# Final norm of a one-core kernel: the addition of the loaded rows moved from VectorE to TensorE, with unread products ahead of it

## The chip, the cores and the metric

The kernel runs on one core of one Trainium2 chip. The metric is the device time of one execution in microseconds (us). The median of three runs before the change is 2208.36 us.

## What is computed

The kernel computes one layer (an mLSTM and a differential attention side by side, then a mixture of 32 experts) over 1024 rows of 1024 numbers, and a final norm. Only the end matters here:

```python
h = h + moe(u2, ...)              # sum over four experts a row of gate * (act @ w_down[e] + b_down[e])
return rms_norm(h, final_g)

def rms_norm(x, g):
    xf = x.astype(jnp.float32)
    y = xf * lax.rsqrt(jnp.mean(xf * xf, axis=-1, keepdims=True) + EPS)
    return (y * g.astype(jnp.float32)).astype(x.dtype)
```

All inputs and the output are float32.

## The kernel before

The 1024 rows are cut into eight tiles (t = 0 to 7) of 128 rows. The products of the experts, without the bias of the second matrix, are added by indirect DMAs from GpSimd into the buffer `h_dram` in memory. That bias is left to the very end: for a row it is the sum over the experts of gate times `b_down[e]`, which is a product with the gates of the row.

The end of the program has two blocks. In the last lines of TensorE's part of `experts` eight transposes (L2278) bring the gates into PSUM, ScalarE copies them to SBUF (L2417), and TensorE makes the bias sums of tiles 0 and 1 (`last_biases`, L2667). A bias sum has only 32 rows of the array in use, one for each expert; it is two float32 products of 512 columns, one for each half of the 1024 columns of a tile, and each shows as two records in the trace. Then comes a barrier of all engines (L1978), which also waits for GpSimd to see its last addition into `h_dram` landed.

In `final_norm`, behind the barrier, SyncE issues the loads of all eight tiles of `h_dram` into `h_all` (L2583). The bias sums of up to four tiles stand in PSUM (`sums`, the four pairs of banks, which are all of PSUM); TensorE makes those of tiles 2 to 7, and from tile 4 on each waits until VectorE has read the sums four tiles earlier. For each tile VectorE adds the bias sums to the loaded rows (L2612, `add`), ScalarE squares and sums the rows (L2594) and takes the root (L2596), VectorE takes the reciprocal (L2619) and multiplies the rows by it and by `final_g` (L2621), and SyncE stores the tile (L2586). VectorE's order is add(0), add(1), scale(0), add(2), scale(1), and so on.

Of the kernel before, what the change touches and what calls it, by code (L numbers as in the profile page):

```python
# [11 lines left out]
ACT = mybir.ActivationFunctionType  # L12
ALU = mybir.AluOpType
X = mybir.AxisListType.X

P = 128
SEQ = 1024
D_MODEL = 1024
NT = SEQ // P
# [1230 lines left out]
class Kit:  # L1250
# [6 lines left out]
    def sb(self, name, shape, dt=F32):  # L1257
        return self.ctx.enter_context(self.nc.sbuf_tensor(name, shape, dt))
# [689 lines left out]
def experts(nc, k):  # L1948
# [29 lines left out]
    with ExitStack() as c:  # L1978
        sb = lambda n, s, d=F32: c.enter_context(nc.sbuf_tensor(n, s, d))
        ps = lambda n, s: c.enter_context(nc.psum_tensor(n, s, F32))  # L1980
        bias, raw = k.bias, k.raw
# [17 lines left out]
        ah, al = sb("ah", [P, KT, P], F32R), sb("al", [P, KT, P], F32R)  # L1999
# [13 lines left out]
        a_ps = ps("a_ps", [P, 2, 512])  # L2013
# [116 lines left out]
        def _(pe):  # L2130
            pe.sem_inc(parts_used.sem, parts_used.credit)
            def turn(b):
                for n in range(KT):
                    last = pe.transpose(x_ps[:, n, :], xg[b][:, n * P:(n + 1) * P], k.c["ident"])
                last.then_inc(x_turned.sem, 1)
# [5 lines left out]
            def turn_act(i, g, blocks):  # L2141
                pe.wait_ge(act_ready.sem, act_ready.at(i, g + 1))
                pe.wait_ge(a_low.sem, a_low.at(i, g))
                to = turned if blocks == 1 else x_ps
                for n in range(2 * blocks):
                    last = pe.transpose(to[:, n, :], av[g % 2][:, n * P:(n + 1) * P], k.c["ident"])
                last.then_inc(act_turned.sem, 1)

            def biases(i, g, blocks):
                if g < 2:  # L2150
                    pe.wait_ge(y_read.sem, y_read.at(i, g - 1))
                elif blocks == 2:
                    pe.wait_ge(gate_ready.sem, gate_ready.at(i, g - 1))
                else:
                    pe.wait_ge(gu_read.sem, gu_read.at(i, g - 1))

                for b in range(blocks if g < 4 else 0):
                    pe.matmul(acc[g % 2][b][:, :], sel[:, b, :], bias[:, g * 512:(g + 1) * 512], start=True, stop=False)
# [63 lines left out]
            def products(i, ch, blocks):  # L2222
                if HALF_OF[ch] == 0:
                    biases(i, GROUP_OF[ch], blocks)
                last = first_block(i, ch)
                if blocks == 2:
                    last = second_block(ch)
                last.then_inc(parts_used.sem, 1)

            def item(i, blocks):  # L2230
                pe.wait_ge(x_low.sem, x_low.at(i, 0))
                if blocks == 2:
                    pe.wait_ge(xg_loaded[1].sem, xg_loaded[1].at(i, 16))
                    turn(1)
                else:
                    pe.sem_inc(x_turned.sem, 1)
                pe.wait_ge(sel_ready.sem, sel_ready.at(i, 1))
                if blocks == 2:

                    biases(i, 0, blocks)  # L2240
                    for ch in range(2):
                        first_block(i, ch)
                    pe.wait_ge(x_low.sem, x_low.at(i, 1))
                    for ch in range(2):
                        second_block(ch).then_inc(parts_used.sem, 1)
                    by_weights(i, 2)
                    turn_act(i, 0, blocks)
                    for ch in range(3, 8):
                        by_weights(i, ch)
                else:  # L2250
                    pe.sem_inc(tiles_made.sem, tiles_made.per)
                    for ch in range(8):
                        products(i, ch, blocks)
                        if ch >= 3 and ch % 2 == 1:
                            turn_act(i, (ch - 3) // 2, blocks)
                pe.wait_ge(a_low.sem, a_low.at(i, 2))
                products(i, 8, blocks)
                if blocks == 2:
                    pe.wait_ge(gu_read.sem, gu_read.at(i, 3))
                turn_next(i)  # L2260
                products(i, 9, blocks)
                if blocks == 1:
                    turn_act(i, 3, blocks)
                products(i, 10, blocks)
                products(i, 11, blocks)
                if blocks == 2:
                    pe.sem_inc(act_turned.sem, 3)
# [9 lines left out]
            for t in range(NT):  # L2277
                last = pe.transpose(x_ps[0:N_EXPERTS, t, :], k.gates[:, t * N_EXPERTS:(t + 1) * N_EXPERTS], k.c["ident"])  # L2278
            last.then_inc(k.half_pe, 1)
            pe.wait_ge(k.half_act, 4)  # L2280
            pe.wait_ge(k.fg_loaded.sem, k.fg_loaded.at(0, 32))
            pe.wait_ge(y_read.sem, y_read.at(items, 0))
            for t in range(2):
                last_biases(pe, k, k.sums[:, 2 * t:2 * t + 2, :], t)

        @block.scalar
        def _(act):
# [273 lines left out]
def final_norm(nc, k, out):  # L2561

    S = k.steps
    h_loaded, squares, root, rstd_ready, normed = k.norm_steps
    stored = S("out_stored", 16)
    g_loaded, fg = k.fg_loaded, k.final_g
    with ExitStack() as c:
        sb = lambda n, s, d=F32: c.enter_context(nc.sbuf_tensor(n, s, d))
        ht = sb("h_all", [P, NT, D_MODEL])
        ot = sb("out_all", [P, NT, D_MODEL])  # L2570
        ssq = sb("f_ssq", [P, NT])
        rms = sb("f_rms", [P, NT])
        rstd = sb("f_rstd_col", [P, NT])
        more = c.enter_context(nc.psum_tensor("more_sums", [P, 4, 512], F32))
        sums = [k.sums[:, 0:2, :], k.sums[:, 2:4, :], more[:, 0:2, :], more[:, 2:4, :]]

        made, added = (lambda t: 4 + t), (lambda t: 4 + t)
        block = c.enter_context(nc.Block(no_gpsimd_drain=True))

        @block.sync  # L2580
        def _(sp):
            for t in range(NT):
                sp.dma_start(ht[:, t, :], k.h_dram[t * P:(t + 1) * P, :]).then_inc(h_loaded[t].sem, 16)  # L2583
            for t in range(NT):
                sp.wait_ge(normed.sem, normed.at(1, t + 1))
                sp.dma_start(out[t * P:(t + 1) * P, :], ot[:, t, :]).then_inc(stored.sem, 16)  # L2586
            sp.wait_ge(stored.sem, stored.at(0, 16 * NT))

        @block.scalar
        def _(act):  # L2590
            nc.scalar.preload_act_table(ACT.Sqrt)
            for t in range(NT):
                act.wait_ge(k.half_dve, added(t))
                nc.scalar.activation(ot[:, t, :], ht[:, t, :], ACT.Square, accum_out=ssq[:, t:t + 1]).then_inc(squares.sem, 1)  # L2594
                act.wait_ge(squares.sem, squares.at(1, t + 1))
                nc.scalar.activation(rms[:, t:t + 1], ssq[:, t:t + 1], ACT.Sqrt, scale=1.0 / D_MODEL,  # L2596
                                     bias=k.eps[:, 0:1]).then_inc(root.sem, 1)

        @block.tensor
        def _(pe):  # L2600
            for t in range(2, NT):
                if t >= len(sums):
                    pe.wait_ge(k.half_dve, added(t - len(sums)))
                last_biases(pe, k, sums[t % len(sums)], t)

        @block.vector
        def _(dve):
            def add(t):
                dve.wait_ge(h_loaded[t].sem, h_loaded[t].at(1, 16))
                dve.wait_ge(k.half_pe, made(t))  # L2610
                rows = ht[:, t, :].rearrange("p (a b) -> p a b", b=512)
                dve.tensor_tensor(rows, sums[t % len(sums)], rows, ALU.add).then_inc(k.half_dve, 1)  # L2612

            dve.wait_ge(g_loaded.sem, g_loaded.at(0, 32))
            add(0)
            add(1)
            for t in range(NT):
                dve.wait_ge(root.sem, root.at(1, t + 1))
                dve.reciprocal(rstd[:, t:t + 1], rms[:, t:t + 1]).then_inc(rstd_ready.sem, 1)  # L2619
                dve.wait_ge(rstd_ready.sem, rstd_ready.at(1, t + 1))  # L2620
                dve.scalar_tensor_tensor(out=ot[:, t, :], in0=ht[:, t, :], scalar=rstd[:, t:t + 1], in1=fg[:, :],  # L2621
                                         op0=ALU.mult, op1=ALU.mult).then_inc(normed.sem, 1)
                if t + 2 < NT:
                    add(t + 2)


def back(nc, k, out):
# [34 lines left out]
def last_biases(pe, k, out, t):  # L2662


    for half in range(2):
        at = slice(half * 512, half * 512 + 512)
        last = pe.matmul(out[:, half, :], k.gates_turned[:, t * P:(t + 1) * P], k.b_down[:, at], start=True, stop=True)  # L2667
    last.then_inc(k.half_pe, 1)


def lay_out(inputs):
# [72 lines left out]
```

## Time and profile before

| what | value |
|---|---|
| median of three runs | 2208.36 us |
| the three runs | 2207.04, 2212.03, 2208.36 us |
| the profiled execution, its own time | 2210.34 us |
| span of the profiled execution, first to last instruction | 2208.3 us |
| mean granted TensorE clock over the span | 0.978 |
| TensorE busy over the span | 97% |
| final block, from the barrier's end to the end of the span | 2179.99 to 2208.3 us |

The span is 2.0 us shorter than the own time of the same execution. A granted clock of 1.00 is 2.4 GHz, one of 0.50 is 1.2 GHz; these are the two levels that the trace shows. An x behind a group is the number of its records.

### The profile page before, as it was taken

What the parts mean: (1) busy time and instruction counts of PE and PEld (TensorE: products, weight loads), DVE (VectorE), ACT (ScalarE), POOL (GpSimd) and SP (SyncE); (2) the same over time, 40 slices, a digit from 0 to 9 for tenths busy, and PEclk for the clock granted to TensorE, in tenths of its full rate; (3) what the DMA queues carried; (4) which work ended last, traced back from release to release, by engine and by line L of the source; (5) the groups of instructions that cost most, each with busy time, mean ns of one, the idle gap of its engine ahead of it and who ended that gap; (6) DMA issues with size and microseconds to landing.
All of it is one profiled execution on the core that took longest, in us unless ns stands there. A gap on an engine that the chain in (4) does not pass through costs nothing. (4 is left out here: it accounts for less than half of the span.)

```text
span 2208.3 us, 35903 instructions
## 1 busy us (share of the span) xinstructions
PE 2133.2 (97%) x11230; PEld 1811.5 (82%) x11231; DVE 1706.5 (77%) x2127; ACT 1373.6 (62%) x1752; POOL 408.2 (18%) x436
## 2 busy tenths in 40 slices
PE   7999999988959999999999999999999999999998
PEld 7987777767848998898898898988889998889884
DVE  5426667776658777979979978779997778998897
ACT  4324655544447566757857757567775667776675
POOL 0000000002342121213213213212321222221120
PEclk9999999999969999999999999999999999999996
DMA  4111101207859776979979979669997769998897
GB/s 162 44 48 34 58 34 44 101 31 229 181 185 343 248 241 248 377 265 349 382 263 353 377 259 352 236 243 380 373 382 267 252 229 332 388 364 336 290 370 283
DMA packets 106797, 548.41 MB, mean 248 GB/s; under 512 B 18071, under 2 KB 28824, under 8 KB 51834
## 3 DMA queue, kind: packets, MB, share of 16 engines
q1 hardware_dynamic: 88138, 504.89, 61.2%
q0 software_dynamic: 18608, 42.85, 8.1%
q8 instruction: 31, 0.51, 0.1%
q14 instruction: 20, 0.16, 0.0%
HBM read 516.45 MB, written 41.47 MB: 253 GB/s over the span
## 5 line engine op out<-in xcount | busy, mean ns | idle before, releaser
L2431 DVE TENSOR_TENSOR wl<-raw,wh 128x2048 fp32r<-128x2048 f32 x423 | 959.1, 2287 | 44.0 <-PE sums L2188 26.8
L2292 ACT ACTIVATE wh<-raw 128x2048 fp32r<-128x2048 f32 x425 | 804.7, 1912 | 113.2 <-PE sums L2188 39.4
L2172 PE MATMUL sums<-wh,xx 128*128 128x512 f32 x832 | 325.8, 392 | 0.9 <-issue 0.9
L2171 PE MATMUL sums<-wl,xx 128*128 128x512 f32 x832 | 325.6, 391 | 0.0
L2170 PE MATMUL sums<-wh,xx 128*128 128x512 f32 x832 | 325.3, 391 | 0.0
L2103 POOL DMA_INDIRECT h_dram<-y,pairs_mine x47 | 120.8, 2570 | 769.1 <-DVE y L2525 449.2
L2170 PE MATMUL sums<-wh,al 128*128 128x512 f32 x560 | 226.7, 405 | 0.6 <-DVE al L2516 0.3
L2172 PE MATMUL sums<-wh,ah 128*128 128x512 f32 x560 | 219.1, 391 | 0.0
L2171 PE MATMUL sums<-wl,ah 128*128 128x512 f32 x560 | 218.5, 390 | 0.0
L2171 PEld LDWEIGHTS sums<-wl,xx 128*128 128x128 f32 x832 | 156.9, 189 | 34.0
L2172 PEld LDWEIGHTS sums<-wh,xx 128*128 128x128 f32 x832 | 156.7, 188 | 33.4
L2170 PEld LDWEIGHTS sums<-wh,xx 128*128 128x128 f32 x832 | 157.1, 189 | 32.4 <-issue 1.2
L2216 PE MATMUL sums<-xx,wh 128*128 128x384 f32 x576 | 172.2, 364 | 0.0
L2217 PE MATMUL sums<-xx,wl 128*128 128x192 f32 x576 | 144.8, 251 | 0.0
L2172 PEld LDWEIGHTS sums<-wh,ah 128*128 128x128 f32 x560 | 105.1, 188 | 23.1
L2170 PEld LDWEIGHTS sums<-wh,al 128*128 128x128 f32 x560 | 105.2, 188 | 21.4 <-DVE al L2516 2.5
L2171 PEld LDWEIGHTS sums<-wl,ah 128*128 128x128 f32 x560 | 105.5, 188 | 19.0
L131 PE MATMUL unit_ps<-u_high,wc_l 128*128 128x512 f32 x288 | 118.5, 411 | 0.9 <-PEq L215 0.9
L2339 ACT ACTIVATE tg<-tg 128x256 f32<-128x256 f32 (+2 forms) x140 | 64.6, 461 | 88.0 <-DVE tg L2450 71.4
L2216 PE MATMUL a_ps<-xx,wh 128*128 128x384 f32 x384 | 114.4, 363 | 0.0
L133 PE MATMUL unit_ps<-u_high,wc_h 128*128 128x512 f32 x288 | 112.9, 392 | 0.0
L132 PE MATMUL unit_ps<-u_low,wc_h 128*128 128x512 f32 x288 | 112.4, 390 | 0.0
(402 smaller groups left out, 4174.6 us busy)
## 6 DMA issues: line engine op xcount, KB each, us to landing
raw<-in_w_experts SPq DMA_DIRECT2D x426, 1024.0 KB, 6.5
raw<-in_w_chan SPq DMA_DIRECT2D x20, 512.0 KB, 3.3
o_gate<-in_x SPq DMA_DIRECT2D x8, 512.0 KB, 5.9
raw<-in_w_out SPq DMA_DIRECT2D x8, 512.0 KB, 5.5
ht<-in_x SPq DMA_DIRECT2D x8, 512.0 KB, 5.9
h_dram<-ht SPq DMA_DIRECT2D x8, 512.0 KB, 9.0
u_dram<-ut SPq DMA_DIRECT2D x8, 512.0 KB, 10.1
h_all<-h_dram SPq DMA_DIRECT2D x8, 512.0 KB, 6.8
```

Source lines behind the costliest of these rows:

```text
L131: pe.matmul(out, ll, rh, start=start, stop=False)
L132: pe.matmul(out, lh, rl, start=False, stop=False)
L133: return pe.matmul(out, lh, rh, start=False, stop=stop)
L2103: pool.indirect_dma_start(out=k.h_dram, out_offset=bass.IndirectOffsetOnAxis(ap=mine[rows, b, 0:1].bitcast(U32), axis=0), in_=y[rows, b, : ...
L2170: pe.matmul(out, lo[:, n, :], w_hi[:, kk, :], start=g >= 4 and n == 0, stop=False)
L2171: pe.matmul(out, hi[:, n, :], w_lo[:, kk, :], start=False, stop=False)
L2172: last = pe.matmul(out, hi[:, n, :], w_hi[:, kk, :], start=False, stop=half == 1 and kk == 3)
L2216: pe.matmul(out[:, 0:2 * ROWS], w_hi[:, kk, own], xx[:, n, :], start=n == 0, stop=False)
L2217: last = pe.matmul(out[:, 0:ROWS], w_lo[:, kk, own], xx[:, n, 0:ROWS], start=False, stop=n == KT - 1)
L2292: nc.scalar.activation(wh[ch % HIGHS][:, :, :], raw[ch % RAW][:, :, :], ACT.Copy).then_inc(h_split.sem, 1)
L2339: nc.scalar.activation(t, t, ACT.Silu, scale=ALPHA).then_inc(sig_ready.sem, 1)
L2431: dve.tensor_tensor(wl[ch % LOWS][:, :, :], raw[ch % RAW][:, :, :], wh[ch % HIGHS][:, :, :], ALU.subtract).then_inc(l_split.sem, 1)
```

## The change

TensorE, not VectorE, adds the loaded rows to the bias sums: the sums are left open (`stop=False`), and for each half of a tile a product of the identity matrix with 512 columns of the loaded rows is added into the same PSUM bank (`add_rows`). ScalarE and VectorE then read the finished rows out of PSUM. The addition on VectorE is gone, and `h_all` is only loaded, no longer written back. A pair of PSUM banks is free for the bias sums of a later tile only when VectorE has scaled the tile (`normed`), not when it has been added. In front of the barrier TensorE gets 10 products behind the gates' transposes and 16 behind the bias sums of tiles 0 and 1, whose result nobody reads (`keep_busy`).

```diff
+            def keep_busy(n):
+
+                for _ in range(n):
+                    pe.matmul(a_ps[:, 1, :], ah[:, 0, :], bias[:, 0:512], start=True, stop=True)
...
             last.then_inc(k.half_pe, 1)
+            keep_busy(10)
             pe.wait_ge(k.half_act, 4)
...
             for t in range(2):
                 last_biases(pe, k, k.sums[:, 2 * t:2 * t + 2, :], t)
+            keep_busy(16)
...
             for t in range(NT):
-                act.wait_ge(k.half_dve, added(t))
-                nc.scalar.activation(ot[:, t, :], ht[:, t, :], ACT.Square, accum_out=ssq[:, t:t + 1]).then_inc(squares.sem, 1)
+                act.wait_ge(k.half_pe, made(t))
+                nc.scalar.activation(ot[:, t, :], rows(t), ACT.Square, accum_out=ssq[:, t:t + 1]).then_inc(squares.sem, 1)
...
-            for t in range(2, NT):
-                if t >= len(sums):
-                    pe.wait_ge(k.half_dve, added(t - len(sums)))
-                last_biases(pe, k, sums[t % len(sums)], t)
+            def add_rows(t):
+
+                pe.wait_ge(h_loaded[t].sem, h_loaded[t].at(1, 16))
+                for half in range(2):
+                    last = pe.matmul(sums[t % len(sums)][:, half, :], k.c["ident"], ht[:, t, half * 512:half * 512 + 512],
+                                     start=False, stop=True)
+                last.then_inc(k.half_pe, 1)
+
+            for t in range(2, len(sums)):
+                last_biases(pe, k, sums[t], t)
+            for t in range(NT):
+                add_rows(t)
+                if 1 <= t <= NT - len(sums):
+                    pe.wait_ge(normed.sem, normed.at(1, t))
+                    last_biases(pe, k, sums[t - 1], t - 1 + len(sums))
...
-            add(0)
-            add(1)
             for t in range(NT):
                 dve.wait_ge(root.sem, root.at(1, t + 1))
                 dve.reciprocal(rstd[:, t:t + 1], rms[:, t:t + 1]).then_inc(rstd_ready.sem, 1)
                 dve.wait_ge(rstd_ready.sem, rstd_ready.at(1, t + 1))
-                dve.scalar_tensor_tensor(out=ot[:, t, :], in0=ht[:, t, :], scalar=rstd[:, t:t + 1], in1=fg[:, :],
+                dve.scalar_tensor_tensor(out=ot[:, t, :], in0=rows(t), scalar=rstd[:, t:t + 1], in1=fg[:, :],
                                          op0=ALU.mult, op1=ALU.mult).then_inc(normed.sem, 1)
-                if t + 2 < NT:
-                    add(t + 2)
...
     for half in range(2):
         at = slice(half * 512, half * 512 + 512)
-        last = pe.matmul(out[:, half, :], k.gates_turned[:, t * P:(t + 1) * P], k.b_down[:, at], start=True, stop=True)
-    last.then_inc(k.half_pe, 1)
+        pe.matmul(out[:, half, :], k.gates_turned[:, t * P:(t + 1) * P], k.b_down[:, at], start=True, stop=False)
```

How the instructions of TensorE stand at the end of `experts`, between the gates' transposes (`x_ps`) and the barrier's branch, before (-) and after (+); `b_down` and `raw` (the turned gates) are the operands of the bias sums, and L2667 has become L2676:

```order
-L2276 ISA
-L2278 MATMUL x_ps<-cons,gates 32x128 x8
-L2282 REGISTER_ALU
-L2667 MATMUL sums<-b_down,raw 128x512 x4
+L2281 ISA
+L2283 MATMUL x_ps<-cons,gates 32x128 x8
+L2233 MATMUL a_ps<-bias,ah 128x512 x10
+L2288 REGISTER_ALU
+L2676 MATMUL sums<-b_down,raw 128x512 x4
+L2233 MATMUL a_ps<-bias,ah 128x512 x16
```

The unread products (`a_ps`) stand on both sides of the four bias products. Next, TensorE in `final_norm`, from the barrier's branch on, the first rows of the new order (`cons` holds the identity, `h_all` the loaded rows):

```order
 L1978 UNCONDITIONAL_BRANCH
-L2599 UNCONDITIONAL_BRANCH
-L2667 MATMUL more_sums<-b_down,raw 128x512 x4
-L2667 MATMUL sums<-b_down,raw 128x512 x4
-L2667 MATMUL more_sums<-b_down,raw 128x512 x4
-L2567 UNCONDITIONAL_BRANCH
+L2607 UNCONDITIONAL_BRANCH
+L2676 MATMUL more_sums<-b_down,raw 128x512 x4
+L2613 MATMUL sums<-h_all,cons 128x512 x4
+L2676 MATMUL sums<-b_down,raw 128x512 x2
+L2613 MATMUL more_sums<-h_all,cons 128x512 x2
+L2676 MATMUL sums<-b_down,raw 128x512 x2
```

Twelve products have become 28: the same twelve bias products, and sixteen identity products (L2613) between and behind them; the bias sums of tile 4 stand behind the rows of tile 1 and ahead of the rows of tile 2. Last, VectorE at the end of `final_norm` before, and at its start after:

```order
-L2612 TENSOR_TENSOR h_all<-more_sums,h_all 128x1024
-L2619 RECIPROCAL f_rstd_col<-f_rms 128x1
-L2621 SCALAR_TENSOR_TENSOR out_all<-h_all,f_rstd_col,final_g 128x1024
-L2619 RECIPROCAL f_rstd_col<-f_rms 128x1
-L2621 SCALAR_TENSOR_TENSOR out_all<-h_all,f_rstd_col,final_g 128x1024
-L2567 UNCONDITIONAL_BRANCH
+L2625 UNCONDITIONAL_BRANCH
+L2630 RECIPROCAL f_rstd_col<-f_rms 128x1
+L2632 SCALAR_TENSOR_TENSOR out_all<-sums,f_rstd_col,final_g 128x1024
+L2630 RECIPROCAL f_rstd_col<-f_rms 128x1
+L2632 SCALAR_TENSOR_TENSOR out_all<-sums,f_rstd_col,final_g 128x1024
```

VectorE has lost the eight additions and reads PSUM in the scaling.

## Rows read from the trace of the kernel before

**Rows 1.** The chain that ended last, in order of time: start us, us, what.

```profile
2180.03 7.16 PE more_sums L2667 x8
2187.19 6.83 PE sums L2667 x8
2194.02 6.84 PE more_sums L2667 x8
...
2200.95 1.24 DVE h_all L2612
...
2202.21 1.16 ACT out_all L2594 x2
...
2203.92 1.28 DVE out_all L2621
```

**Rows 2.** Stretches: us, PE, PEld, DVE, ACT, POOL busy; granted clock, DMA share, GB/s.

```profile
2169.20:2173.40 4.20, 1.52 (x10) 0.97 (x9) 3.29 (x2) 3.43 (x4) 2.43 (x1) 1.00 0.04 18
2173.50:2179.60 6.10, 6.10 (x8) 1.89 (x6) 0.00 (x0) 0.00 (x0) 0.56 (x1) 0.50 0.55 86
2179.00:2180.00 1.00, 0.60 (x1) 0.00 (x0) 0.00 (x0) 0.01 (x1) 0.00 (x0) 0.50 0.00 0
2180.00:2200.90 20.90, 20.81 (x24) 7.80 (x24) 16.33 (x19) 11.27 (x22) 0.00 (x0) 0.50 0.87 326
```

**Rows 3.** Timeline from the gates' transposes on: start us, us, engine, group [idle before].

```profile
2169.21 1.03 PE L2278 MATMUL x_ps<-cons,gates 128*32 128x128 f32 x8
2170.97 3.09 POOL L2103 DMA_INDIRECT h_dram<-y,pairs_mine  x1 [13.56 <-ACT y L2360]
2172.92 6.67 PE L2667 MATMUL sums<-b_down,raw 32*128 32x512 f32 x8 [2.68 <-ACT raw L2417]
2175.13 0.33 PEld L2667 LDWEIGHTS sums<-b_down,raw 32*128 32x128 f32 x1 [0.53 <-issue]
2175.99 0.33 PEld L2667 LDWEIGHTS sums<-b_down,raw 32*128 32x128 f32 x1 [0.53 <-issue]
2180.00 3.80 SPq L2583 DMA_DIRECT2D h_all<-h_dram  x8
2183.78 2.44 DVE L2612 TENSOR_TENSOR h_all<-sums,h_all 128x1024 f32<-128x1024 f32 x2 [11.29 <-PE more_sums L2667]
```

**Rows 4.** Last indirect addition (L2103) of the end: time to landing.

```profile
DMA to landing us min/median/max: 7.6/7.6/7.6
```

**Rows 5.** Timeline of two earlier stretches, TensorE alone.

```profile
502.34 0.63 PE L133 MATMUL o_ps<-wo_h,mh 128*128 128x512 f32 x1
502.77 0.63 PE L131 MATMUL o_ps<-wo_h,ml 128*128 128x512 f32 x1
...
504.66 0.40 PE L133 MATMUL o_ps<-wo_h,mh 128*128 128x512 f32 x1
504.89 0.39 PE L131 MATMUL o_ps<-wo_h,ml 128*128 128x512 f32 x1
```

**Rows 6.** Float32 products on 128 rows, at the two levels of the clock.

```profile
478.77 1.72 PE L848 MATMUL sk_ps<-tok,pdT 128*128 128x128 f32 x14
484.65 3.78 PE L848 MATMUL sk_ps<-tok,pdT 128*128 128x128 f32 x16 [0.69 <-ACT pdT L950]
```

**Rows 7.** Stretches between earlier changes of the clock, columns as in rows 2.

```profile
494.20:500.90 6.70, 0.00 (x0) 0.00 (x0) 2.57 (x4) 2.52 (x3) 0.00 (x0) 0.50 0.62 168
501.00:504.30 3.30, 2.95 (x7) 2.40 (x8) 3.30 (x5) 2.46 (x4) 0.00 (x0) 0.50 0.93 324
504.40:507.70 3.30, 3.30 (x16) 2.71 (x15) 3.30 (x4) 3.30 (x4) 0.00 (x0) 1.00 1.08 398
511.20:514.60 3.40, 2.70 (x12) 1.89 (x11) 1.29 (x2) 0.85 (x1) 1.23 (x1) 1.00 0.82 157
514.60:517.90 3.30, 1.45 (x6) 1.21 (x7) 1.23 (x1) 0.16 (x1) 3.10 (x4) 1.00 0.28 103
518.10:521.40 3.30, 3.30 (x10) 2.53 (x9) 1.60 (x2) 1.09 (x3) 3.23 (x2) 0.50 0.99 399
```

**Rows 8.** Groups by line and form that read PSUM: busy us, mean ns.

```profile
L2306 ACT ACTIVATE xx<-x_ps 128x1024 fp32r<-128x1024 f32 x36 | 36.6, 1018 | 34.6 <-PE x_ps L2134 34.6
L2525 DVE SCALAR_TENSOR_TENSOR y<-sums,pairs_mine,hh 64x512 f32<-64x512 f32 x24 | 17.8, 742 | 52.7 <-ACT hh L2370 52.7
```

More of the change, by code:

```diff
@@ L2575, in final_norm @@
         sums = [k.sums[:, 0:2, :], k.sums[:, 2:4, :], more[:, 0:2, :], more[:, 2:4, :]]
-        made, added = (lambda t: 4 + t), (lambda t: 4 + t)
+        made = lambda t: 4 + t
+        rows = lambda t: sums[t % len(sums)].rearrange("p a b -> p (a b)")
         block = c.enter_context(nc.Block(no_gpsimd_drain=True))
@@ L2600, in _ @@
         def _(pe):
-            for t in range(2, NT):
-                if t >= len(sums):
-                    pe.wait_ge(k.half_dve, added(t - len(sums)))
-                last_biases(pe, k, sums[t % len(sums)], t)
+            def add_rows(t):
[11 more added lines that the diff above has]
+                    last_biases(pe, k, sums[t - 1], t - 1 + len(sums))
         @block.vector
         def _(dve):
[L2608 to L2612, printed above, removed]
             dve.wait_ge(g_loaded.sem, g_loaded.at(0, 32))
-            add(0)
-            add(1)
             for t in range(NT):
```

## The prediction

> **What bounds the kernel now.** I read the chain that ended last first. Over the final block it is TensorE: 24 records of bias sums without a pause from 2180.03 to 2200.86, then VectorE's addition of tile 7, ScalarE's square and root, VectorE's scaling, which ends at 2205.20 [rows 1], and a store of 3.1 us to the end of the span. Next the stretches, for the clock. TensorE stood at 1.00 until the gates' transposes were through, idled until ScalarE had the turned gates ready, and has stood at 0.50 since about 2173.5, through 6.10 and 20.81 us of bias sums in which it hardly paused [rows 2]. So products on 32 rows, however dense, did not bring the clock back here. A record of a bias sum takes 0.86 us at this level (weight loads at 2175.13 and 2175.99) [rows 3]; a tile, four records, takes 3.4.
>
> The barrier: TensorE's last record ends at 2179.60 [rows 2] and the final block begins at 2179.99. GpSimd would allow it earlier: its last addition is issued at 2170.97 and lands 7.6 us later, at 2178.6 [rows 3, 4]. So TensorE sets the barrier too, by 1.0 us.
>
> **Prices.** A float32r product of 512 columns starts every 0.43 us at 0.50 and every 0.23 at 1.00 [rows 5], a factor of 0.53. For a float32 record of 512 columns at 1.00 that gives 0.86 x 0.53 = 0.46; a float32 record of 128 columns takes (1.72 - 0.17) / 13 = 0.12 there and (3.78 - 0.17) / 15 = 0.24 at 0.50 [rows 6] (0.17 is a guess at the last one's drain), so 0.48 by length; exact halving of 0.86 gives 0.43. I take 0.44 us a record, 1.76 a tile. The identity products are float32 on 128 rows, as those of rows 6 are, and I give them the same two records a product, so 1.76 a tile too. In the final block TensorE then has 6 + 8 = 14 tile units where it had 6: 24.6 us at full clock, against 20.5 now at half clock. It is more work even if the clock is held throughout; at half clock it is 48.
>
> **The change part by part.**
>
> *The 10 unread products.* They run from about 2170.1, behind the transposes, for 10 x 0.23 = 2.3 us to 2172.4; the bias sums can't start before 2172.92, when the turned gates are there [rows 3]. Cost nothing, hidden behind ScalarE; without that cover 2.3 us.
>
> *Bias sums of tiles 0 and 1 and the 16 behind.* At full clock 8 x 0.44 = 3.5 us to 2176.4, then 16 x 0.23 = 3.7 to 2180.1, and the last one's drain: 2180.3, against 2179.60. So even then the barrier comes 0.7 us later, to about 2180.65: the 16 take back all that the bias sums won, and the loads of `h_all` behind the barrier start later by it.
>
> *In the final block, at full clock, from its start.* Bias sums of tiles 2 and 3 until 3.55. Tile 0 lands at 3.79 (VectorE's first addition, 2183.78 - 2179.99) [rows 3]; its identity products run to 5.55, those of tile 1 to 7.3. Now the new wait: the bias sums of tile 4 need tile 0 scaled. From the end of a tile's last product to its scaling's end are 0.3 for drain and handing over and 2205.20 - 2202.21 = 2.99 for square, root, reciprocal and scaling [rows 1], together 3.3, so 8.85. TensorE idles 1.55, and the rows of tiles 2 and 3, whose bias sums are ready and which have landed by then, stand behind that wait in its queue; ScalarE waits for them. Behind it bias sums of 4, rows of 2, and so on to rows of 5 are 8 units, 14.1 us, to 22.95 (the later waits are met: rows of tile 1 end at 7.3, scaled at 10.6, needed at 12.4), and rows of tiles 6 and 7 go to 26.5. Plus 3.3: 29.8 for the last scaling, against 2205.20 - 2179.99 = 25.2 now. So +4.6, which already has the removed addition (1.24 and a hand-over) in it. VectorE's eight additions elsewhere are worth nothing, since it waited for TensorE.
>
> *ScalarE and VectorE on PSUM.* The square of 1024 columns out of SBUF takes 1.06 [rows 1], a ScalarE copy of as many out of PSUM 1.02; the scaling out of PSUM lies between the 1.28 of SBUF and twice the 0.74 of 512 columns, 1.48 [rows 8]. I take no change; at the last tile alone it could cost 0.2.
>
> Sum at full clock throughout: 0.7 + 4.6 = +5.3 us.
>
> *The clock.* Only in part will it be held. The trace has two falls with the engine at work: it fell at 518.0, after a stretch with products for 1.45 of 3.30 us, and it did not fall after one with 2.70 of 3.40; it rose at 504.35 after 2.95 of 3.30 on 128 rows [rows 7]. The low stretch at 518.1 to 521.4, busy throughout on 128 rows, is the shortest: what ran in its 3.3 us would have taken 1.75 at full clock, so one costs about 1.6 us. The change has two thin places like that at 514.6: the 3.5 us of bias sums on 32 rows in front of the 16 unread products (which on 128 rows should raise it again), and the 1.55 us of waiting with 1.76 of bias sums behind it. I take the first as sure and the second as even: 1.6 + 0.8 = +2.4. Both ends: +0 and, if it stays low in the whole final block, 14 x 1.65 = +23.
>
> Together +7.7 us. The sum is made against the profiled execution, 2210.34, which gives 2218.0; that is 2.0 above the median of the runs shown, so beside the median it is 2216. What can be told from no change is about 0.2%, 4.4 us.
>
> **The rivals.**
>
> *The clock is held throughout* (0.20). For it: the engine never idles long, and on 128 rows the clock rises. Against it: 20.81 busy us on 32 rows at 0.50 [rows 2]. Then +5.3: 2213.6, own range 2212 to 2215. The Trainium skill, "TensorE: Matmul & The Clock Gate", section "Why this matters for your kernels", asks only that TensorE be kept busy without long gaps for the full clock, and would give this case. The trace disagrees for the kernel before, as just shown.
>
> *The clock falls in the final block and stays low over most of the alternation* (0.20). Bias sums and rows alternate there, half of the time on 32 rows, and only the rows of 5, 6 and 7 stand together. For it: low, the 32-row products last twice as long. Against it: the rows of tiles 0 and 1 stand together and should raise it first. If all eight units from the bias sums of 4 to the rows of 5 run low: 5.3 + 1.6 + 8 x 1.65 = +20, 2228; half of them, 2222.
>
> *Not slower: the identity products are cheap* (0.08). If one took only a float32r product's 0.23 [rows 5], a tile's rows would be 0.46. Rows of 0 end at 4.25, it is scaled at 7.55, then bias 1.76 and rows 0.46 alternate to 16.4, rows of 6 and 7 follow at once, ScalarE takes its last three tiles 1.4 apart, and the last scaling ends near 22.5: -2.7 + 0.7, 2206.3. It decides from about 1.1 us a tile down. Against it: these are float32, as rows 6. The Trainium skill, "FP8 and Floating Point Precision", counts four passes for a true float32 product, which speaks for the dear price; no row here shows an identity product of this width.
>
> *The likeliest, as summed* (0.50): 2216, own range 2212.5 to 2220. The last 0.02 is for what I don't see.
>
> **How the numbers follow.** Faster by over 0.2% wants under 2204: a part of the cheap case and runs that scatter, 0.05. Within 0.2%: the rest of that case, some 0.06 each of the held clock and of the likeliest (runs of one kernel scatter by 5 us), 0.17. Slower 0.78. The range takes in the likeliest, the held clock and the nearer half of the low one: 2211 to 2227.
>
> **What would show it.** In the changed profile: identity products as two records each, of 0.43 to 0.46 us spacing at 1.00; TensorE's last record before the barrier at 2180.3 or later; TensorE waiting about 1.5 us for VectorE's scaling of tile 0, once; the final block from barrier to last scaling at 30 us or more; the granted clock at 1.00 in most of it, with one or two low stretches, one of them from within the bias sums of 0 and 1 or just behind. I am wrong if the identity products have one record, if the clock counts bias sums as work enough, or if it stays at 0.50 to the end.

## The result

The changed kernel takes 2217.39 us (median of 10 runs, 2213.25 to 2222.30), the kernel before 2208.64 (10 runs, 2205.71 to 2212.03): a ratio of 1.0036, 95% interval 1.0027 to 1.0045. It is slower by 8.8 us; forecast were 2216 and a loss of 7.7 us against the same execution.

The profiled execution has a span of 2215.5 us. What comes ahead of the gates' transposes is the same work in both kernels and varies by some microseconds between executions (in the traces of this study the transposes begin between 2163.2 and 2170.4), so I compare from the transposes' start to the end of the span: 2208.3 - 2169.21 = 39.1 us before [rows 3], 2215.5 - 2168.81 = 46.7 after, +7.6. The timeline of TensorE of the changed kernel from there on, in start, us, group [idle before]:

```profile
2168.81 1.04 PE L2283 MATMUL x_ps<-cons,gates 128*32 128x128 f32 x8
2169.60 2.57 PE L2233 MATMUL a_ps<-bias,ah 128*128 128x512 f32 x10
2172.53 3.69 PE L2676 MATMUL sums<-b_down,raw 32*128 32x512 f32 x8 [0.36 <-ACT raw L2424]
2176.15 3.94 PE L2233 MATMUL a_ps<-bias,ah 128*128 128x512 f32 x16
2180.51 3.67 PE L2676 MATMUL more_sums<-b_down,raw 32*128 32x512 f32 x8 [0.41 <-PEq L1978]
2184.14 5.40 PE L2613 MATMUL sums<-h_all,cons 128*128 128x512 f32 x8
2190.62 1.98 PE L2676 MATMUL sums<-b_down,raw 32*128 32x512 f32 x4 [1.08 <-DVE out_all L2632]
2192.53 1.98 PE L2613 MATMUL more_sums<-h_all,cons 128*128 128x512 f32 x4
...
2205.82 3.60 PE L2613 MATMUL more_sums<-h_all,cons 128*128 128x512 f32 x8
```

The bias sums of tiles 0 and 1 take 3.7 us where they took 6.7 [rows 3], and the 16 unread products behind them take it all back: the final block begins 11.7 us behind the start of the transposes, before 10.8. The identity products have two records each, as many columns as a bias sum, and TensorE waits once, 1.08 us, for the scaling of tile 0. Then a unit of four records starts every 1.91 us.

Stretches of the same execution (us; PE, PEld, DVE, ACT, POOL busy; granted clock, DMA share, GB/s):

```profile
2176.20:2180.00 3.80, 3.80 (x17) 2.88 (x16) 0.00 (x0) 0.00 (x0) 0.00 (x0) 1.00 0.30 59
2180.60:2184.00 3.40, 3.40 (x8) 1.28 (x8) 0.00 (x0) 1.15 (x1) 0.00 (x0) 1.00 0.71 246
2184.70:2188.00 3.30, 3.30 (x5) 1.35 (x4) 0.00 (x0) 0.46 (x1) 0.00 (x0) 0.50 1.00 391
2190.60:2205.90 15.30, 15.28 (x33) 5.63 (x34) 5.79 (x8) 4.61 (x11) 0.00 (x0) 1.00 0.46 185
```

The clock fell once, behind the bias sums of tiles 2 and 3, and came back during the identity products. Over most of the final block it stands at 1.00, where it stood at 0.50 before [rows 2], and the block is longer all the same. VectorE, which set the pace before (b_unread_128rows below shows it), is busy for 5.79 of 15.30 us. The chain that ended last (start, us, what) closes like this:

```profile
2205.99 3.45 PE more_sums L2613 x8
2209.43 0.02 issue
2209.46 1.12 ACT out_all L2602 x2
...
2210.93 0.17 DVE f_rstd_col L2630
...
2211.13 1.28 DVE out_all L2632
```

From the block's start, 2180.47, to the end of the last scaling, 2212.41, are 31.9 us; before they were 25.2.

### The profile page after: what moved, and what is told of

It is laid out like the page before. It is cut to its first block and busy times, and to the rows that moved or that the text cites. A ratio compares the mean times of both kernels' runs of the same rounds, so it can differ in the third digit from the quotient of the medians.

```text
span 2215.5 us, 36004 instructions
## 1 busy us (share of the span) xinstructions
PE 2143.6 (97%) x11288; PEld 1817.4 (82%) x11289; DVE 1698.1 (77%) x2119; ACT 1373.2 (62%) x1752; POOL 405.6 (18%) x436
## 5 line engine op out<-in xcount | busy, mean ns | idle before, releaser
L2103 POOL DMA_INDIRECT h_dram<-y,pairs_mine x47 | 120.7, 2568 | 780.9 <-DVE y L2532 454.7
```

The costliest lines, as they stand in the source:

```text
L2103: pool.indirect_dma_start(out=k.h_dram, out_offset=bass.IndirectOffsetOnAxis(ap=mine[rows, b, 0:1].bitcast(U32), axis=0), in_=y[rows, b, : ...
```

## Experiments

Each was run 6 to 12 times and stands beside 23 to 30 runs of the kernel before on the same chip (the first row has the 10 and 10 runs above); "tail" is the time from the start of the transposes to the end of the span in its profiled execution (before 39.1, changed 46.7), "block" from the final block's start to the end of the last scaling (25.2 and 31.9).

| kernel | median us | ratio to before, 95% | tail | block |
|---|---|---|---|---|
| changed | 2217.39 | 1.0036, 1.0027 to 1.0045 | 46.7 | 31.9 |
| b_unread | 2212.82 | 1.0013, 1.0002 to 1.0025 | 39.4 | 24.6 |
| b_unread_128rows | 2210.64 | 0.9997, 0.9986 to 1.0008 | 40.3 | 24.8 |
| a_no_unread | 2219.80 | 1.0048, 1.0031 to 1.0064 | 49.6 | 35.4 |
| a_no_16 | 2218.95 | 1.0038, 1.0026 to 1.0050 | 48.7 | 35.8 |
| a_128rows | 2215.74 | 1.0029, 1.0017 to 1.0040 | 43.8 | 29.2 |
| a_rows_first | 2216.21 | 1.0025, 1.0014 to 1.0036 | 47.1 | 30.8 |
| a_128rows_no_rows | 2208.42 | 0.9993, 0.9982 to 1.0004 | 39.2 | 24.7 |
| mixed | 2204.06 | 0.9974, 0.9961 to 0.9986 | 34.9 | 21.9 |
| mixed_32rows | 2215.18 | 1.0024, 1.0011 to 1.0036 | 44.8 | 30.3 |
| b_10_8_128rows | 2210.13 | 0.9999, 0.9989 to 1.0010 | 38.7 | 24.8 |

### What was the bound before, and what the clock was worth there

b_unread is the kernel before with the unread products alone:

```diff
             last.then_inc(k.half_pe, 1)
+            keep_busy(10)
...
                 last_biases(pe, k, k.sums[:, 2 * t:2 * t + 2, :], t)
+            keep_busy(16)
```

> The kernel before with only the 10 and 16 unread products added; VectorE still adds the loaded rows. Theory (TensorE's added work is what costs, and before VectorE was the bound of the final block at 2.53 us a tile, TensorE only at the last tile by 0.3 us): the clock is at 1.00 in front of the barrier, which comes 0.5 to 0.9 us later; in the final block the bias sums on 32 rows let it fall to 0.50 and nothing brings it back; time 2208 to 2210, no difference from before. Rival (the clock was the bound before): holding it halves 20.8 us of bias sums, so up to 10 us less, 2199.

b_unread_128rows has in addition zero rows under `b_down`, so that a bias product has the same result and uses all rows of the array (the other operand is read over all its 128 rows, of which the last 96 meet zeros):

```diff
-        k.b_down = ... nc.sbuf_tensor("b_down", [N_EXPERTS, D_MODEL], F32, side="right")
+        k.b_down = ... nc.sbuf_tensor("b_down", [P, D_MODEL], F32, side="right")
...
+            for r in range(1, 4):
+                dve.memset(k.b_down[r * N_EXPERTS:(r + 1) * N_EXPERTS, :], 0.0)
...
-        k.gates_turned[:, t * P:(t + 1) * P], k.b_down[:, at]
+        k.raw_store[0][:, t * P:(t + 1) * P], k.b_down[:, at]
```

> The kernel before with the unread products and with bias products on 128 rows; VectorE still adds. Theory: the clock stays at 1.00 through the final block, the bias sums take 1.72 us a tile, TensorE waits for VectorE's additions, VectorE stays at 2.53 us a tile and the time at 2207 to 2210, no difference from before. Rival (TensorE at half clock was the bound before): several us less, down to 2199.

In b_unread the clock stands at 1.00 until 2182.7 and at 0.50 from there on, through the bias sums of the final block; in b_unread_128rows it stays up until 2196.1, when TensorE has long finished. TensorE's timeline of the two, b_unread first:

```profile
2184.22 7.19 PE L2674 MATMUL sums<-b_down,raw 32*128 32x512 f32 x8 [1.01 <-DVE h_all L2619]
2191.21 7.03 PE L2674 MATMUL more_sums<-b_down,raw 32*128 32x512 f32 x8
```

```profile
2184.66 3.70 PE L2676 MATMUL sums<-b_down,raw 128*128 128x512 f32 x8 [1.32 <-DVE h_all L2621]
2188.82 1.98 PE L2676 MATMUL more_sums<-b_down,raw 128*128 128x512 f32 x4 [0.46 <-DVE h_all L2621]
2191.35 1.98 PE L2676 MATMUL more_sums<-b_down,raw 128*128 128x512 f32 x4 [0.54 <-DVE h_all L2621]
```

Eight records take 7.2 us in the one and 3.7 in the other, and the block is 24.6 and 24.8 us long. The chain of both goes through VectorE, one addition every 2.53 us (b_unread, start, us, what):

```profile
2192.16 1.22 DVE h_all L2619
...
2194.68 1.22 DVE h_all L2619
```

So before the change VectorE was full too, and a TensorE twice as fast is worth 0.4 to 0.6 us: the rival of both is out. That b_unread is slower by 0.13% I did not expect, and its profiled execution shows only 0.3 us of it (tail 39.4). The unread products can cost more in executions in which the clock falls ahead of them, as a_rows_first shows below. The profiled execution is the fastest of the twelve and at the top of their mean granted clocks (0.983 of 0.980 to 0.983), which fits; but where the others were low isn't shown.

### What the unread products are worth in the changed kernel

a_no_unread is the changed kernel with neither group, a_no_16 with the 10 alone (`keep_busy(16)` taken out).

> The changed kernel without both groups of unread products. Theory: the clock is at 0.50 when the final block begins, the bias sums of tiles 2 and 3 take 6.8 us instead of 3.6, the rows of tiles 0 and 1 on 128 rows bring it back to 1.00 within or just behind them; the barrier is 0.5 to 0.9 us earlier; together 3 to 5 us slower than the changed kernel, 2220 to 2223. Rival 1: once low it stays low while bias sums and rows alternate, 15 to 20 us slower, 2232 to 2238. Rival 2: the unread products do nothing for the clock, 2216.5.

> The changed kernel with the 10 unread products and without the 16. Theory (the 16 set the barrier and hold the clock for the bias sums behind it): barrier 1.5 to 1.9 us earlier, set by GpSimd's last addition; the clock falls before or at the barrier, bias sums of tiles 2 and 3 at 0.50 cost 3.4 us more and the rows of tile 0 part of that again; 1 to 3 us slower than the changed kernel, 2218 to 2220.5. Rival (the 16 buy nothing): 1.5 us faster, 2216.

In a_no_unread the clock fell at 2171.4 and stayed down until 2188.4; in a_no_16 from 2172.2 until 2185.9. TensorE of a_no_unread:

```profile
2178.68 7.16 PE L2674 MATMUL more_sums<-b_down,raw 32*128 32x512 f32 x8 [0.41 <-PEq L1978]
2185.77 5.03 PE L2611 MATMUL sums<-h_all,cons 128*128 128x512 f32 x8
2192.20 1.98 PE L2674 MATMUL sums<-b_down,raw 32*128 32x512 f32 x4 [1.41 <-DVE out_all L2630]
```

The bias sums of tiles 2 and 3 take 7.2 us instead of 3.7, and the rows of tiles 0 and 1 bring the clock back, as forecast; tail +2.9, a little under the 3 to 5 expected; the median is +2.4, but the intervals of the two ratios overlap, so it is the trace that carries this. It did not stay low over the alternation. The 16 alone: without them TensorE is through earlier and waits 2.47 us at the barrier, the block starts 9.8 us behind the transposes instead of 11.7, and loses more than that to the lower clock (35.8 us against 31.9); tail +2.0, the medians within each other's spread. So the unread products do buy something in the changed kernel, 2 to 3 us by the traces, and it is less than the 6.7 us by which the block grew.

### The rows of the array: clock and weight loads

a_128rows is the changed kernel with the zero rows of b_unread_128rows.

> The changed kernel, with zero rows under b_down so that the bias products use all 128 rows of the array (the same sums). Theory (32-row products are what lets the clock fall, and the change between 32-row and 128-row products exposes 0.19 us of weight load each time): clock 1.00 from the transposes to the last product, a tile unit 1.72 us instead of 1.91, final block from barrier to last scaling about 29.3 us instead of 31.9, median 2214 to 2215. Rival (neither hangs on the rows): still one low stretch of about 3.4 us near the bias sums and 1.91 a unit, 2217.

The clock is at 1.00 from the transposes to beyond the last product, and a unit starts every 1.72 us:

```profile
2187.05 1.98 PE L2678 MATMUL sums<-b_down,raw 128*128 128x512 f32 x4 [1.41 <-DVE out_all L2634]
2188.87 1.88 PE L2615 MATMUL more_sums<-h_all,cons 128*128 128x512 f32 x4
2190.58 1.88 PE L2678 MATMUL sums<-b_down,raw 128*128 128x512 f32 x4
2192.30 1.88 PE L2615 MATMUL more_sums<-h_all,cons 128*128 128x512 f32 x4
```

In the changed kernel the first weight load of each unit starts together with the unit, behind an idle time, and the same load is hidden in a_128rows. The changed kernel's timeline of loads:

```profile
2192.53 0.30 PEld L2613 LDWEIGHTS more_sums<-h_all,cons 128*128 128x128 f32 x2 [0.76 <-issue]
...
2194.44 0.29 PEld L2676 LDWEIGHTS sums<-b_down,raw 32*128 32x128 f32 x2 [0.76 <-issue]
```

Four records are 1.72 us, the change of rows adds 0.19. From the start of the bias sums of tile 4 to the end of the rows of tile 5, seven such changes, that makes 15.2 us, where a_128rows takes 13.8. The block is 29.2 us, where the full-clock sum of the prediction had 29.8. Here is the change with its clock held all through: it still is 0.29% slower than before. The median, 2215.74, lies between theory and rival, and its interval overlaps that of the changed kernel; what the rows are worth here, 2.9 us of tail, is read from the traces.

### The wait on the scaled tile

a_rows_first takes the identity products of tile 2 ahead of the first wait, and every later bias sum one tile later:

```diff
-                if 1 <= t <= NT - len(sums):
-                    pe.wait_ge(normed.sem, normed.at(1, t))
-                    last_biases(pe, k, sums[t - 1], t - 1 + len(sums))
+                if 2 <= t <= NT - len(sums) + 1:
+                    pe.wait_ge(normed.sem, normed.at(1, t - 1))
+                    last_biases(pe, k, sums[t - 2], t - 2 + len(sums))
```

> The changed kernel with the identity products of tile 2 ahead of the first wait for a scaled tile, and each later bias sum one tile later in the queue. Theory (the wait for tile 0 to be scaled holds up rows that could run): TensorE no longer idles at that wait, the final block is 1.1 to 1.5 us shorter at the same clock, 2216. Rival (that idle time only shifts to the next wait): the wait comes back at the bias sums of tile 5 and the time is that of the changed kernel, 2217.4.

TensorE, with the clock at 0.50 from 2174.1 to 2177.5 and from 2184.3 to 2187.7:

```profile
2174.66 5.28 PE L2233 MATMUL a_ps<-bias,ah 128*128 128x512 f32 x16
2180.36 3.67 PE L2676 MATMUL more_sums<-b_down,raw 32*128 32x512 f32 x8 [0.41 <-PEq L1978]
2183.95 5.40 PE L2613 MATMUL sums<-h_all,cons 128*128 128x512 f32 x8
2189.19 1.88 PE L2613 MATMUL more_sums<-h_all,cons 128*128 128x512 f32 x4
2191.00 1.98 PE L2676 MATMUL sums<-b_down,raw 32*128 32x512 f32 x4
```

The idle time is gone and has not come back elsewhere; the block is 1.2 us shorter, the median too. The timed difference alone is within the intervals; the trace shows it. This execution also has the fall that the prediction held for sure: within the bias sums of tile 1. The 16 unread products then take 5.28 us instead of 3.94 and the block starts 13.2 us behind the transposes.

### The identity products themselves

a_128rows_no_rows is a_128rows with the identity products cut to 8 of 512 columns, so it leaves out the addition of the loaded rows, and keeps waits and order. With `start=True` the 8 columns hold the loaded rows in place of the bias sums; the bias products are closed with `stop=True`:

```diff
-                    last = pe.matmul(sums[t % len(sums)][:, half, :], k.c["ident"], ht[:, t, half * 512:half * 512 + 512],
-                                     start=False, stop=True)
+                    last = pe.matmul(sums[t % len(sums)][:, half, 0:8], k.c["ident"], ht[:, t, half * 512:half * 512 + 8],
+                                     start=True, stop=True)
```

> The changed kernel with 128-row bias products, whose identity products are cut to 8 of 512 columns, so the loaded rows are left out of the output but for those columns; waits and order as before. Theory (the identity products' own time is the cost): TensorE's units of rows nearly vanish, the bias sums of 4 to 7 follow each other from the scaling of tile 0 on, the final block from barrier to last scaling is about 18 us instead of 29.3, 2204 to 2206. Rival (the waits on scaled tiles are the cost, whatever the rows take): less than 4 us gained, above 2212.

The block is 24.7 us: 4.5 shorter than a_128rows, where I expected 11 and the rival under 4. Both were too simple. The timeline of TensorE:

```profile
2185.98 3.02 PE L2678 MATMUL sums<-b_down,raw 128*128 128x512 f32 x4 [1.84 <-DVE out_all L2634]
2188.80 0.86 PE L2615 MATMUL more_sums<-h_all,cons 128*128 128x8 f32 x4
2189.51 2.29 PE L2678 MATMUL sums<-b_down,raw 128*128 128x512 f32 x4
2191.64 0.51 PE L2615 MATMUL more_sums<-h_all,cons 128*128 128x8 f32 x4
2192.70 1.98 PE L2678 MATMUL more_sums<-b_down,raw 128*128 128x512 f32 x4 [0.56 <-DVE out_all L2634]
```

The rows of tile 2 stand behind the bias sums of tile 4, and those of 6 behind the scaling of 2, so a loop of rows, square, root, scaling and bias sums is closed through TensorE's queue; and the engine, now idle for 1.84 us ahead of it, lost its clock from 2186.7 to 2190.1 (1.7 us). So the identity products' own time and the order of the change overlap: with the clock's 1.7 taken off, 6.2 us of the 13.8 that eight tiles of rows take come back. The prediction's rival of cheap identity products, which had this order in its sum, had the block at 22.5 us, near the 23.0 that are left without the clock's 1.7.

### Sharing the additions

Before, VectorE is full and TensorE could have room; after, the reverse. In mixed TensorE adds the rows of the odd tiles and VectorE those of the even ones, with 128-row bias products and 8 unread products instead of 16:

```diff
+        by_pe = (1, 3, 5, 7)
+        order = [('bias', 2), ('bias', 3), ('rows', 1), ('bias', 4), ('rows', 3), ('bias', 6), ('bias', 5), ('rows', 5), ('bias', 7), ('rows', 7)]
+        dve_order = [('add', 0), ('add', 2), ('scale', 0), ('scale', 1), ('add', 4), ('scale', 2), ('scale', 3), ('add', 6), ('scale', 4), ('scale', 5), ('scale', 6), ('scale', 7)]
...
-            keep_busy(16)
+            keep_busy(8)
```

> TensorE adds the rows of tiles 1, 3, 5, 7, VectorE those of tiles 0, 2, 4, 6; bias products on 128 rows; 10 and 8 unread products. Theory (before, VectorE was full at 2.53 us a tile; changed, TensorE is full at 3.8): with the additions shared neither is, the final block takes about 22 us to the last scaling instead of 25.2, the barrier is set by GpSimd; 3 to 4 us faster than before, 2205.5. Rival (other waits take their place, or the clock falls in the gaps): within 1.5 us of before, 2208 to 2211.

It takes 2204.06 us, 0.26% less than before (0.9974, 0.9961 to 0.9986), and its block 21.9 us, as worked out. Stretches of its execution, then its chain that ended last, from the landing of tile 1 on (start, us, what):

```profile
2168.00:2179.00 11.00, 10.04 (x40) 6.28 (x39) 4.43 (x3) 4.60 (x6) 3.09 (x1) 1.00 0.37 72
2179.00:2201.00 22.00, 17.67 (x40) 7.42 (x40) 15.64 (x20) 12.45 (x25) 0.00 (x0) 1.00 0.91 354
```

```profile
2183.90 1.98 PE sums L2632 x4
2185.88 1.72 PE sums L2705 x4
...
2196.18 1.73 PE more_sums L2632 x4
...
2199.61 1.28 DVE out_all L2661
```

TensorE is busy for 17.67 of 22.00 us and VectorE for 15.64. That neither is full, as the theory had it, holds only over the whole block: from 2183.90 to 2197.91 the chain is eight units of TensorE without a pause. TensorE sets the pace here too; it has four tiles of rows fewer than in the changed kernel, 6.9 us. The block starts 9.8 us behind the transposes, as in a_no_16, TensorE waiting. Two controls, each with one part of it undone: mixed_32rows has bias products on 32 rows, b_10_8_128rows lets VectorE add all tiles.

> The shared additions and 10 and 8 unread products, but the bias products on 32 rows as in the changed kernel. Theory: 0.19 us of weight load at each of the seven or eight changes between 32-row and 128-row products and one low stretch of the clock (about 1.7 us) come back, 2206.5 to 2208. Rival (sharing alone is the gain, TensorE has room): as with 128 rows, 2204.

> The kernel before with everything of the shared version but the sharing: bias products on 128 rows, 10 and 8 unread products, VectorE adds all tiles. Theory (VectorE at 2.53 us a tile is the bound): final block 25 us from barrier to last scaling, only the barrier about 1 us earlier than before, 2207.5 to 2209. Rival (the shared version's gain is the barrier and the clock): 2204 to 2205.

b_10_8_128rows is where the kernel before is (0.9999), block 24.8: barrier and clock alone are not the gain, sharing (with the order of work that it has) is. But mixed_32rows is slower by 0.24%, worse than expected. Its clock is at 0.50 from 2177.9 to 2181.3, from 2184.7 to 2198.3 and from 2201.8 to 2205.2:

```profile
2186.50 3.78 PE L2630 MATMUL sums<-h_all,cons 128*128 128x512 f32 x4 [0.41 <-DMA h_all<-h_dram]
2190.21 3.77 PE L2703 MATMUL sums<-b_down,raw 32*128 32x512 f32 x4
2193.92 3.78 PE L2630 MATMUL more_sums<-h_all,cons 128*128 128x512 f32 x4
2197.63 2.34 PE L2703 MATMUL more_sums<-b_down,raw 32*128 32x512 f32 x4
```

That is the rival of the prediction in which the clock stays low while bias sums and rows alternate, seen in a relative of the change. The timed executions agree: the twelve of mixed_32rows have mean granted clocks of 0.980 to 0.985, the two fastest (2208.63 and 2210.01 us) the two highest, and those of mixed 0.986 to 0.989. 96 rows of zeros are worth 0.5% there.

## Why the prediction was right

*The bound before.* Right in part. The chain named TensorE, and I said that VectorE's additions were worth nothing to remove since it waited for TensorE. It waited for the first tile's load, once 0.3 us for ScalarE's root, and for TensorE only 0.3 us, at the last tile: 16.33 us of work between 2183.78 and 2200.9 stood in [rows 2, 3], and I did not read them together. b_unread_128rows shows it full at 2.53 us a tile. Nothing in the sum hung on it, since it was TensorE's new work that was counted, but removing VectorE's additions was half of a good change, and I had written it off.

*The 10 unread products.* Hidden, as said: they end at 2172.2, the bias sums start at 2172.53.

*Barrier.* Said 0.7 us later at full clock; measured 11.7 against 10.8 from the transposes, 0.9.

*Final block at full clock.* Said 29.8; a_128rows, with the clock held, has 29.2. The price of a record was 0.44 and is 0.43, two records for an identity product were right. What the sum lacked is the 0.19 us of weight load at each change between 32 and 128 rows. The block of the changed kernel has nine changes; two stand behind waits, for the landing of tile 0 and for its scaling, and the other seven cost 1.4 us.

*The new wait.* Said 1.55 us of idle time once; 1.08, 1.41 in a_128rows, where nothing is low. That the rows of tile 2 stand behind it without need is shown by a_rows_first.

*PSUM reads.* The square out of PSUM takes 1.02 us and the scaling 1.28 (1.06 and 1.28 out of SBUF): no change, as taken.

*The clock.* Right in kind. I held a fall at the first thin place for sure and at the second for even. In the profiled execution neither came, but one I had not named: right behind the bias sums of tiles 2 and 3, a third thin place. In a_rows_first, whose work up to there is the same, the clock fell at the first place and at this one. So the +2.4 was one stretch of 1.7 here. The sum of 7.7 lacked 1.4 for weight loads and 0.2 for the barrier. It had 0.5 too much for the block at full clock (29.8 against 29.2), 0.7 too much for the clock, and 0.3 for the wait, which the low stretch shortened (1.08 against 1.41). That it met 7.6 is partly luck. The medians differ by 8.8, the two profiled executions by 7.2.

*The rivals.* The clock held throughout: a_128rows makes it, 43.8 of tail, +4.7 instead of +5.3. Staying low did not happen in the changed kernel's trace but does in mixed_32rows; nor does it seem to have happened in its other timed executions, which have no trace. Half of the eight units of that rival at half clock would be 14 us at 0.50 and lower the mean granted clock by 0.003; the ten have 0.985 to 0.988, the traced one 0.986. One more short low stretch can't be told that way. Cheap identity products: two records each, so no.

## What to carry to other kernels

Count work on the engine that takes it over before asking whether its clock can be held: eight tiles of float32 identity products were 13.8 us at full clock for an engine that had 10.3 to do. Where two engines are both close to the pace, share the added work between them rather than move it, and find out first which of them is full by making only the other faster (as b_unread_128rows does). If an engine works through thin products, look at the granted clock beside its busy time: filling the unused rows with zeros changed nothing in the sums and was worth 11 us in the shared version, 2.9 us of tail in the changed kernel, and nothing where VectorE was full (blocks of 24.6 and 24.8).

## What the runs showed of the hardware that was not expected

A change between float32 products on 32 rows and on 128 rows exposes a weight load of 0.19 us (units of 1.91 us against 1.72 with all rows in use). Dense products on 32 rows did not keep the clock at 1.00: it fell at 2182.7 in b_unread and stayed at 0.50 through 14 us of them. In b_unread_128rows, which differs in the rows alone (most of them zeros), the same products ran at 1.00 to the end although TensorE paused before them (1.32, 0.46 and 0.54 us), and so they did in a_128rows and in mixed.
